# Each expert's rows chosen on three lists of 512 affinities side by side on 96 partitions

## The reference, cut to what matters

```python
def expert_choice_ffn(x, w_router, w_gate, w_up, w_down):
    b, s, d = x.shape
    T = b * s
    cap = CAPACITY_FACTOR * T // N_EXPERTS          # 64 for the prompt, 128 for the sample
    h = x.reshape(T, d)
    aff = jax.nn.softmax((h @ w_router).astype(jnp.float32), axis=-1)
    gate_vals, tok_idx = lax.top_k(aff.T, cap)      # per expert, over all tokens of the sequence
    xg = h[tok_idx]
    hid = jax.nn.silu(jnp.einsum('ecd,edf->ecf', xg, w_gate)) * jnp.einsum('ecd,edf->ecf', xg, w_up)
    out = jnp.einsum('ecf,efd->ecd', hid, w_down) * gate_vals[..., None].astype(x.dtype)
    y = jnp.zeros_like(h).at[tok_idx.reshape(-1)].add(out.reshape(-1, d))
    return y.reshape(b, s, d)
```

## Time and profile before

| | us |
|---|---|
| median of 3 runs | 3817.47 |
| lowest and highest of the 3 | 3811.43, 3818.25 |
| the profiled execution's own time | 3811.89 |
| its span in the profile | 3810.1 |

### The profile page before, as it was taken

The page is one execution under the profiler, slowest core; times in us unless marked ns, Lnnn a source line. Parts: engine busy times, 40 slices in busy tenths (PEclk is TensorE's granted clock), DMA queues, the critical chain, the costliest instruction groups (busy, mean ns, idle before and its releaser), DMA issues. The chain is left out here.

```text
span 3810.1 us, 62111 instructions
## 1 busy us (share of the span) xinstructions
PE 3494.3 (92%) x20180; PEld 3089.1 (81%) x20180; DVE 2418.0 (63%) x3972; ACT 1824.8 (48%) x3108; POOL 443.2 (12%) x399
## 2 busy tenths in 40 slices
PE   8999698785980899999999999999999999999993
PEld 6888687563540889899898998998989989899993
DVE  6421166785558667667676676766767667577674
ACT  3222265110110556556565565655656556556564
POOL 0010153432330000000000000000000000000002
PEclk9999899786995899999999999999999999999996
DMA  4221333113220777777777777777777777777775
GB/s 160 78 67 65 74 88 90 35 31 110 98 87 13 240 231 234 238 236 229 235 237 227 235 231 234 235 231 232 229 237 235 227 233 234 223 236 222 237 236 185
DMA packets 238842, 688.84 MB, mean 181 GB/s; under 512 B 52608, under 2 KB 68768, under 8 KB 238400
## 3 DMA queue, kind: packets, MB, share of 16 engines
q1 hardware_dynamic: 222240, 628.47, 51.4%
q0 software_dynamic: 15552, 54.72, 5.3%
q10 hardware_dynamic: 864, 3.15, 0.2%
HBM read 635.81 MB, written 50.43 MB: 180 GB/s over the span
## 5 line engine op out<-in xcount | busy, mean ns | idle before, releaser
L1723 PE MATMUL moe_gu<-moe_xgT,moe_whi 128*128 128x384 f32 x5632 | 1626.1, 362 | 7.1 <-issue 3.5
L1855 DVE TENSOR_TENSOR moe_wlo<-moe_raw,moe_whi 128x1024 fp32r<-128x1024 f32 x1056 | 1290.0, 1223 | 480.2 <-ACT moe_whi L1809 476.8
L1724 PE MATMUL moe_gu<-moe_xgT,moe_wlo 128*128 128x192 f32 x5632 | 1410.5, 250 | 0.0
L1809 ACT CAST moe_whi<-moe_raw 128x1024 fp32r<-128x1024 f32 x1056 | 1106.0, 1048 | 484.2 <-PE moe_dnp L1739 389.1
L1724 PEld LDWEIGHTS moe_gu<-moe_xgT,moe_wlo 128*128 128x128 f32 x5632 | 1078.9, 192 | 0.4
L1723 PEld LDWEIGHTS moe_gu<-moe_xgT,moe_whi 128*128 128x128 f32 x5632 | 1060.5, 188 | 12.3 <-issue 4.8
L1816 ACT COPY moe_part<-moe_gu 128x384 f32<-128x384 f32 x352 | 168.7, 479 | 449.0 <-PE moe_gu L1724 437.5
L1861 DVE TENSOR_TENSOR moe_guv<-moe_gu,moe_part 128x384 f32<-128x384 f32 x352 | 196.2, 557 | 282.9 <-ACT moe_part L1816 281.3
L1688 POOL DMA_INDIRECT tmp_acc<-moe_og_s,moe_srow_s x16 | 25.8, 1614 | 2263.2 <-ACT moe_og_s L1841 2263.2
L1735 PE MATMUL moe_dns<-moe_whi,moe_hid 128*128 128x512 f32 x704 | 275.9, 392 | 0.0
L1738 PE MATMUL moe_dnp<-moe_whi,moe_hid 128*128 128x512 f32 x704 | 275.6, 392 | 0.0
(11 more groups left out here) (258 smaller groups left out, 4117.2 us busy)
## 6 DMA issues: line engine op xcount, KB each, us to landing
moe_raw<-in_w_ffn SPq DMA_DIRECT2D x1056, 512.0 KB, 3.9
prj_wraw<-in_w_in SPq DMA_DIRECT2D x12, 1024.0 KB, 5.3
att_raw<-tmp_qkT SPq DMA_DIRECT2D x32, 384.0 KB, 6.9
prj_share<-in_xT SPq DMA_DIRECT2D x6, 1024.0 KB, 10.4
tmp_qkT<-prj_share POOLq DMA_DIRECT2D x24, 256.0 KB, 2.7
ssd_xb<-tmp_xbc SPq DMA_DIRECT2D x12, 512.0 KB, 3.9
mix_xr<-in_x SPq DMA_DIRECT2D x12, 512.0 KB, 3.7
tmp_h<-mix_h POOLq DMA_DIRECT2D x12, 512.0 KB, 3.0
```

The source lines that it names most:

```text
L1723: pe.matmul(out[:, a, 0:2 * CAP], whi[c][:, j, :], x, start=(j == 0), stop=False)
L1724: mm = pe.matmul(out[:, a, 0:CAP], wlo[c][:, j, :], x[:, 0:CAP], start=False, stop=(j == KD - 1))
L1809: act.copy(whi[c][:], raw[c][:]).then_inc(hi_done, 1)
L1855: dve.tensor_tensor(wlo[c][:], raw[c][:], whi[c][:].bitcast(F32), ALU.subtract).then_inc(lo_done, 1)
```

## The change

The 1536 affinities of an expert are no longer one line with two parts, but three lists of 512, which stand side by side on partitions 0 to 15 (first half of the sample), 32 to 47 (second half) and 64 to 79 (prompt). The partitions between them hold zeros. One round now handles all three lists, over 96 partitions and 512 columns, and there are 16 rounds, since either half of the sample can hold all 128 of its largest.

Each half then has its 128 largest in falling order. Of the two, with the second reversed, the larger of each pair at the same place is taken: these are the 128 largest of both (one step of a bitonic merge). The prompt's first 64 are taken from its 128.

To bring the lists to their partitions, three VectorE copies place `aff` in a tile `wide` of 96 columns per 128 tokens, which is set to zero at the start of the mix stage, and four transposes of `wide` take the place of twelve of `aff`. The merge is done behind the transposes at the end, with tokens' places on the partitions. `affT` is now 96 partitions of 512 (2 KB on a partition, and 6 KB before), and `wide` takes 1.5 KB on a partition in the mix stage; the tiles of the experts stage are what they were.

```diff
+SPAN = 512
+LISTS, LIST = TOK // SPAN, 32
...
-            pe.wait_ge(aff_ready, 1 + NT)
-            for t in range(NT):
-                bank = (trA, trB, hrA)[t // 4]
-                mm = pe.transpose(bank[0:EXPERTS, t % 4, :], aff[:, t, :], ident[:])
+            pe.wait_ge(wide_ready, 1 + LISTS)
+            for j in range(SPAN // P):
+                mm = pe.transpose(trA[0:LISTS * LIST, j, :], wide[:, j, :], ident[:])
             mm.then_inc(at_mm, 1)
...
+            dve.memset(wide[:], 0.0).then_inc(wide_ready, 1)
+            dve.wait_ge(wide_ready, 1)
             dve.wait_ge(const_in, 80)
...
             tiles(dve, body)
+            dve.wait_ge(aff_ready, 1 + NT)
+            per = SPAN // P
+            for n, q in enumerate((1, 2, 0)):
+                dve.tensor_copy(wide[:, :, LIST * n:LIST * n + EXPERTS], aff[:, per * q:per * q + per, :]).then_inc(wide_ready, 1)
             dve.wait_ge(at_mm, 1)
-            for b, bank in enumerate((trA, trB, hrA)):
-                dve.tensor_copy(res["affT"][:, 512 * b:512 * b + 512], bank[0:EXPERTS].rearrange("e j t -> e (j t)")).then_inc(at_done, 1)
-            dve.wait_ge(at_done, 3)
+            dve.tensor_copy(res["affT"][:], trA[0:LISTS * LIST].rearrange("e j t -> e (j t)")).then_inc(at_done, 1)
+            dve.wait_ge(at_done, 1)
...
-            n = 0
-            for q, c0, cap in parts:
-                work = res["affT"][:, sum(SEQS[:q]):sum(SEQS[:q]) + SEQS[q]]
-                for r in range(cap // 8):
...
-            dve.tensor_scalar(idxf[:, 0:CAPS[1]], idx[:, 0:CAPS[1]], float(SEQS[0]), None, ALU.add).then_inc(float_ready, 1)
-            dve.tensor_copy(idxf[:, CAPS[1]:], idx[:, CAPS[1]:]).then_inc(float_ready, 1)
+            work = res["affT"][:]
+            for r in range(HALF // 8):
+                at = slice(8 * r, 8 * r + 8)
+                dve.max(val[:, at], work).then_inc(step, 1)
+                dve.wait_ge(step, 3 * r + 1)
+                dve.max_index(idx[:, at], val[:, at], work).then_inc(step, 1)
+                dve.wait_ge(step, 3 * r + 2)
+                dve.match_replace(work, val[:, at], work, -1.0).then_inc(step, 1)
+                dve.wait_ge(step, 3 * r + 3)
+
+            dve.tensor_scalar(rowa[:], idx[A:A + EXPERTS, :], float(SEQS[0]), None, ALU.add).then_inc(lists_ready, 1)
+            dve.tensor_copy(valb[:], val[B:B + EXPERTS, ::-1]).then_inc(lists_ready, 1)
+            dve.tensor_scalar(rowb[:], idx[B:B + EXPERTS, ::-1], float(SEQS[0] + SPAN), None, ALU.add).then_inc(lists_ready, 1)
+            dve.tensor_copy(valp[:], val[PR:PR + EXPERTS, 0:CAPS[0]]).then_inc(lists_ready, 1)
+            dve.tensor_copy(rowp[:], idx[PR:PR + EXPERTS, 0:CAPS[0]]).then_inc(lists_ready, 1)
             dve.wait_ge(tr_mm, 1)
-            for i, (q, c0, cap) in enumerate(parts):
-                dve.tensor_copy(res["gates"][i][:], ps[0:cap, 2 * i, :]).then_inc(done, 1)
-                dve.tensor_copy(res["rows"][i][:], ps[0:cap, 2 * i + 1, :]).then_inc(done, 1)
-            dve.wait_ge(done, 4)
+            dve.tensor_copy(tok[:], ps[:, 0:4, :]).then_inc(done, 1)
+            dve.tensor_copy(res["gates"][1][:], ps[0:CAPS[0], 4, :]).then_inc(done, 1)
+            dve.tensor_copy(res["rows"][1][:], ps[0:CAPS[0], 5, :]).then_inc(done, 1)
+            dve.wait_ge(done, 3)
+            dve.tensor_tensor(res["gates"][0][:], tok[:, 0, :], tok[:, 2, :], ALU.max).then_inc(done, 1)
+            dve.tensor_tensor(first[:], tok[:, 0, :], tok[:, 2, :], ALU.is_ge).then_inc(done, 1)
+            dve.tensor_tensor(diff[:], tok[:, 1, :], tok[:, 3, :], ALU.subtract).then_inc(done, 1)
+            dve.wait_ge(done, 6)
+            dve.tensor_tensor(diff[:], diff[:], first[:], ALU.mult).then_inc(done, 1)
+            dve.wait_ge(done, 7)
+            dve.tensor_tensor(res["rows"][0][:], diff[:], tok[:, 3, :], ALU.add).then_inc(done, 1)
+            dve.wait_ge(done, 8)
...
+            one = ident[0:EXPERTS, 0:EXPERTS]
+            for n, of in enumerate((val[A:A + EXPERTS, :], rowa[:], valb[:], rowb[:])):
+                pe.transpose(ps[:, n, :], of, one)
+            pe.transpose(ps[0:CAPS[0], 4, :], valp[:], one)
+            pe.transpose(ps[0:CAPS[0], 5, :], rowp[:], one).then_inc(tr_mm, 1)
```

More of the change, by code:

```diff
@@ L1189, in stage_mix @@
         aff = m.sb("aff", [P, NT, EXPERTS])
+        wide = m.sb("wide", [P, SPAN // P, LISTS * LIST])
         a2 = [m.sb(f"a2{s}", [P, HEADS, HD]) for s in range(2)]
@@ L1237, in stage_mix @@
         at_done = m.sem("at_done")
+        wide_ready = m.sem("wide_ready")
         a2_in = m.sems("a2_in")
@@ L1517, in _ @@
             tiles(dve, body)
+            dve.wait_ge(aff_ready, 1 + NT)
+            per = SPAN // P
+            for n, q in enumerate((1, 2, 0)):
+                dve.tensor_copy(wide[:, :, LIST * n:LIST * n + EXPERTS], aff[:, per * q:per * q + per, :]).then_inc(wide_ready, 1)
             dve.wait_ge(at_mm, 1)
[L1519 to L1521 removed]
+            dve.tensor_copy(res["affT"][:], trA[0:LISTS * LIST].rearrange("e j t -> e (j t)")).then_inc(at_done, 1)
+            dve.wait_ge(at_done, 1)
 def stage_choose(nc, dram, res):
+    HALF = CAPS[1]
+    A, B, PR = 0, LIST, 2 * LIST
     with ExitStack() as ctx:
@@ L1528, in stage_choose @@
         ident = m.sb("ident", [P, P])
[L1529 to L1532, removed]
+        val = m.sb("val", [LISTS * LIST, HALF])
+        idx = m.sb("idx", [LISTS * LIST, HALF], U32)
+        valb = m.sb("valb", [EXPERTS, HALF])
+        valp = m.sb("valp", [EXPERTS, CAPS[0]])
+        rowa = m.sb("rowa", [EXPERTS, HALF])
+        rowb = m.sb("rowb", [EXPERTS, HALF])
+        rowp = m.sb("rowp", [EXPERTS, CAPS[0]])
+        tok = m.sb("tok", [P, 4, EXPERTS])
+        first = m.sb("first", [P, EXPERTS])
+        diff = m.sb("diff", [P, EXPERTS])
+        ps = m.ps("ps", [P, 6, EXPERTS])
         const_in = m.sem("const_in")
         step = m.sem("step")
-        float_ready = m.sem("float_ready")
+        lists_ready = m.sem("lists_ready")
         tr_mm = m.sem("tr_mm")
@@ L1571, in _ @@
             pe.wait_ge(const_in, 16)
-            pe.wait_ge(float_ready, 2)
-            for i, (q, c0, cap) in enumerate(parts):
-                pe.transpose(ps[0:cap, 2 * i, :], val[:, c0:c0 + cap], ident[0:EXPERTS, 0:EXPERTS])
-                mm = pe.transpose(ps[0:cap, 2 * i + 1, :], idxf[:, c0:c0 + cap], ident[0:EXPERTS, 0:EXPERTS])
-            mm.then_inc(tr_mm, 1)
+            pe.wait_ge(lists_ready, 5)
+            one = ident[0:EXPERTS, 0:EXPERTS]
[3 more added lines that the diff above has]
+            pe.transpose(ps[0:CAPS[0], 5, :], rowp[:], one).then_inc(tr_mm, 1)
 def stage_experts(nc, dram, res):
@@ L2005, in residents_later @@
     return {
-        "affT": m.sb("affT", [EXPERTS, TOK]),
+        "affT": m.sb("affT", [LISTS * LIST, SPAN]),
         "att": att,
```

1 line of the change is left out of this document (removed).

## The result

The changed kernel takes 3780.28 us (median of 4 executions, 3775.26 to 3783.65). Beside it the kernel before took 3814.99 us (4 executions, 3811.43 to 3818.25). The ratio is 0.9911, with a 95% interval of 0.9895 to 0.9926: faster, by about 35 us where the forecast said 44.9. The time lies 1.3 us above the forecast's range of 3763 to 3779.

What follows compares the result with a forecast made beforehand. The serial choice of rows on VectorE was taken to bound the kernel ahead of the experts. Rounds -43.8, seam -2.4 and tail +1.3 summed to -44.9 us, giving 3769.8 us, range 3763 to 3779.

Steps and rivals of the forecast that it cites:

- The rounds: Choice of rows on VectorE: 16 rounds of 2.279 us, 36.46 us in place of 80.28, a gain of 43.8 us.
- lists one after another: Rival in the rounds' three passes: 96 partitions worked group by group, 6.84 us a round, 3845 us; 3 in 100.
- half as dear again: Rival in the rounds: on 96 partitions a round takes 3.42 us, giving 3791 us; 3 in 100.
- The seam: From the last affinities to the first MAX8: 2.83 us in place of 5.23, a gain of 2.4 us.
- The tail: From the rounds' end to SyncE's first issue: 3.15 us in place of 1.85, a cost of 1.3 us.
- The memset: Zeroing `wide` at the mix stage's start: 0.4 us, costing nothing because VectorE idles there for the constants.
- TensorE's clock: At the seam and in the tail TensorE goes on working at the lower clock, as now.
- the rival in which it keeps the higher one: Start of the experts: TensorE keeps the higher clock over the shorter gap, at most 6 us less, 3764; 2 in 100.
- Behind the barrier: From SyncE's first issue to the end: same instructions and tiles, the same 2574 us as now, within 5.
- the experts give something back: Rival behind the barrier: more TensorE stalls at the lower clock, 3777 us for two places, 3780 for three; 11 in 100.

Runs made afterwards that it cites:

- x2_pad31: Changed kernel plus 31 idle semaphore increments on VectorE ahead of its expert loop, putting the loop back to its place in the kernel before; 3768.50 us (5 executions).
- y1_pad31: The same kernel as x2_pad31, run again on another chip; 3771.43 us (4 executions).
- shift 0: VectorE's expert loop at its place in the kernel before; here the changed kernel with 31 idle increments on VectorE, median 3769.9 us (9 executions).
- x3_before_pad97: Kernel before, with its old choice of rows, plus 97 idle semaphore increments on VectorE ahead of its expert loop; 3820.48 us (12 executions), ratio 1.0018.
- y3: Changed kernel plus 16 idle semaphore increments on VectorE ahead of its expert loop; 3765.66 us (6 executions).
- z2: The same kernel as y3, run again beside the changed kernel; 3764.57 us (5 executions).
- third job: Follow-up runs of the changed kernel again (3778.17 us) beside versions with 16 or 47 idle increments on VectorE, or 16 there and 31 on ScalarE; kernel before 3813.83 us.
- z4: Changed kernel plus 16 idle semaphore increments on VectorE and 31 on ScalarE; 3769.28 us (5 executions).
- y4_act31: Changed kernel plus 31 idle semaphore increments on ScalarE and none on VectorE; 3773.27 us (6 executions).

## Why the prediction was right ahead of the barrier and wrong behind it

**The rounds: right.** Start to start over 16 of them it is (1189.04 - 1152.19) / 16 = 2.303 us, where 2.279 was forecast; 36.85 us in place of 36.46. The three lists are worked side by side. Between 16 and 96 partitions MAX8 went from 682 to 691 ns, and FIND_INDEX8 by as much, so the price that I set at nothing is 9 ns for such a pass and 24 ns for a round, 0.4 us in all. The rivals of lists one after another and of half as dear again are out.

**The seam: exact.** From 1149.13 + 0.23 to MAX8 at 1152.19 are 2.83 us, and 2.83 was forecast.

**The tail: right, 0.3 us long.** 1192.48 - 1189.04 = 3.44 us, forecast 3.15, within the bounds of 1.0 and 2.9 us of cost (it cost 3.44 - 1.85 = 1.6). The five operations ahead of TensorE took most of it. `valb` started 0.25 us behind `rowa` and `valp` 0.24 behind `rowb`, where `rowb` followed `valb` by 0.14. The Trainium skill's rule of the other group of partitions ("VectorE: DVE Perf Modes", section "Two Vector instructions with no wait between them") gives 0.22 for the first two: by that rule, the trace agrees, and my 0.14 was wrong there.

**The memset and TensorE's clock: right.** 0.38 us, with VectorE idle 2.88 us ahead of it and 6.92 behind it, where I had asked for 8 or more; its next work starts at 900.11, 0.5 us later than before, and the last affinities are as much later. TensorE's four transposes at the seam took 1.09 us, the lower clock. In the first 26 us of the experts, behind the shorter gap, its granted clock is 0.52 (1192.5 to 1218.5 us), so the rival in which it keeps the higher one is out.

These steps gave 44.2 us where 43.8 + 2.4 - 1.3 = 44.9 were forecast; the 0.7 are the rounds' 0.4 and the tail's 0.3.

**Behind the barrier: the step that failed.** The prediction says that what follows "has the same instructions and the same tiles in both kernels", and asks for "the same 2574 us as now ..., within 5". It has the same instructions, but they stand at another place in VectorE's stream. The profile has 2584.4 us for that stretch, 10.5 more, and 2580.0 and 2581.1 in two later ones. With the loop moved back to its place the same choice of rows takes 3813.3 - 3768.5 = 44.8 us off the kernel before in one job (x2_pad31) and 3810.11 - 3771.43 = 38.7 in the other (y1_pad31); the forecast's sum of 44.9 lies near the first, by some luck. Left 31 instructions further ahead, it gives 8.0 us of that back (15 executions of the changed kernel against 9 with shift 0, 3777.9 - 3769.9; resampled, 1.1 to 12.5 us). That loss needs no new choice: x3_before_pad97 lost 7.2 us without it. That the first four executions came out at 3780.28, above the 3777.9 of all 15, is chance.

The rival "the experts give something back" had the right size, 3777 to 3780 us, at 11 in 100, and the wrong cause. I priced it as more places at the lower clock by chance, and such places there are, but a quarter of the loss (2.7 of 11.0 us) is TensorE waiting, and all four falls of the clock within the loop follow turns at which VectorE comes late. The row that could have told me, the count of fetches on queue 14, stands on the page of before; what it would be with 31 instructions fewer ahead of the loop no row of before tells.

The Trainium skill ("Advanced Engine Details and Errata", section "ISA Cache") says that an engine other than TensorE keeps 32 KB of instructions in two lines of 16 KB, 256 instructions each, and that the size can be set per engine. The runs here show the kind of thing and another size: packets of 8 KB, and a pattern that comes back at +128 instructions. Had the place counted within 256 instructions, nothing would have made +97 act like -31 and +128 like 0.

**A version that beats both.** The changed kernel with 16 of these instructions (y3, z2) has a median of 3764.9 us over 11 executions (3759.24 to 3775.03). In the third job it was 3764.57 against 3778.17 for the changed kernel, 13.6 us less, and its ratio to the kernel before is 0.9880 (0.9862 to 0.9898) where that one's is 0.9904 (0.9886 to 0.9922). Over all jobs, 29 executions of kernels with 16, 31 or 47 of them (z4, with ScalarE's 31 besides, among them) have a median of 3768.5 us, 15 of the changed kernel 3777.9: resampled, the difference is 5.0 to 14.1 us.

## What to carry to other kernels

A change ahead of a loop moves the loop in its engine's instruction stream, and on an engine whose late turn others wait for, that alone was worth 7 to 9 us of 3777 here, in a median of many executions: 7.2 lost by the kernel before when its loop was moved, 8.0 and 9.4 gained back by the changed one. Compare the packets of the instruction queues of both pages before you explain a small difference in a part that wasn't touched. Where they differ, run the changed kernel with a few idle instructions ahead of the loop: it takes one edit, and it separates what the change does from where it put the code.

## What the runs showed of the hardware

- MAX8 and FIND_INDEX8 over 512 columns cost nearly nothing for more partitions: 682 and 672 ns on 16, 691 and 681 on 96. MATCH_VALUE_LOAD takes 88 ns on 96.
- Whether VectorE's loop needs some 29 more fetches of 8 KB (67 or 96 packets) hangs on its place, and the pattern comes back after 128 instructions: late at -31, -23, +33 and +97, on time at -15, 0, +16, +25, +128 and +256.
- One semaphore count on VectorE takes 0.096 us in a row of them.
- At its loop's jump ScalarE stands still for 1.8 to 3.5 us in the kernel before, and not at all between two turns.
- A VectorE that is late by 0.4 to 2.3 us once in 314 us can cost TensorE more than the wait: 16.6 us more at the lower clock for 2.7 us more idle in the changed kernel's profile. In y4_act31's it didn't: the turns were late by 0.3 to 1.0 us, and the clock fell at none.
